# Expert rows gathered in quarters and transposed on VectorE: one change to a fused mixer and mixture-of-experts kernel

## The reference, cut to what matters

```python
probs = softmax(x @ w_router)                  # (2048, 16)
# top-1 of 4 expert groups, then top-2 experts within it
gate = take(probs, eidx); gate = gate / sum(gate)
# rows sorted by expert and padded to blocks of 128 rows
hid = silu(xb @ w1[e]) * (xb @ w3[e])          # (128, 512)
y   = hid @ w2[e]                              # (128, 1024)
ffn = sum over the two experts of y * gate
out = layer_norm(ALPHA * h + ffn)
```

## Time and profile before

| What | Value |
|---|---|
| median of 3 runs | 2238.5 us |
| the three runs | 1352.0, 2238.5, 5668.24 us |
| span of the profiled execution | 1348.3 us |
| its own time, span and what lies around it | taken as the lowest run, 1352.0 us (3.7 us more than the span) |
| TensorE busy in the span | 1311.4 us (97%) |
| VectorE, ScalarE, GpSimd busy | 958.4, 511.7, 525.1 us |
| granted clock of TensorE, mean | 0.994 |
| the loop over blocks | from about 650 to 1335 us |

### The profile page before, as it was taken

How to read it: one execution, slowest core, us unless ns; L and a number is a source line. 1 busy time by engine, 2 the same in 40 slices (tenths; PEclk the granted TensorE clock), 3 DMA queues, 4 the chain that set the end, 5 groups by cost and what they waited for, 6 DMA issues and landing times. The chain is left out here.

```text
span 1348.3 us, 20368 instructions
## 1 busy us (share of the span) xinstructions
PE 1311.4 (97%) x6382; PEld 1095.8 (81%) x6383; DVE 958.4 (71%) x1357; ACT 511.7 (38%) x568; POOL 525.1 (39%) x543
## 2 busy tenths in 40 slices
PE   5999999999999999998999999999999999999995
PEld 5888888888888888887888888888888888888884
DVE  7758577687759785698777886665675677776564
ACT  3423234322443234323444454343443454434241
POOL 2001010111101110022566665755665656666555
PEclk9999999999999999999999999999999999999998
DMA  9625434563455344544777774563554545666421
GB/s 266 181 89 162 149 111 163 170 192 109 156 186 158 110 141 159 208 181 169 287 263 256 271 270 147 193 234 132 181 202 181 191 164 214 236 231 238 142 69 64
DMA packets 156522, 243.58 MB, mean 181 GB/s; under 512 B 18944, under 2 KB 84992, under 8 KB 156480
## 3 DMA queue, kind: packets, MB, share of 16 engines
q1 hardware_dynamic: 118624, 154.15, 35.3%
q0 software_dynamic: 28928, 71.74, 15.0%
q10 hardware_dynamic: 8928, 17.13, 3.7%
HBM read 211.97 MB, written 64.62 MB: 205 GB/s over the span
## 5 line engine op out<-in xcount | busy, mean ns | idle before, releaser
L520 PE MATMUL acc<-ring_hi 128*128 128x512 f32 (+1 forms) x800 | 308.8, 386 | 2.1 <-DVE ring_lo L1239 1.9
L522 PE MATMUL acc<-ring_hi,ring_lo 128*128 128x512 f32 (+1 forms) x800 | 305.6, 382 | 0.0
L521 PE MATMUL acc<-ring_lo,ring_hi 128*128 128x512 f32 (+1 forms) x800 | 305.3, 382 | 0.0
L520 PE MATMUL acc<-ring_hi,xt_hi 128*128 128x512 f32 x648 | 256.7, 396 | 4.1 <-issue 2.8
L522 PE MATMUL acc<-ring_hi,xt_lo 128*128 128x512 f32 x648 | 252.8, 390 | 0.0
L521 PE MATMUL acc<-ring_lo,xt_hi 128*128 128x512 f32 x648 | 252.4, 390 | 0.0
L1802 POOL TENSOR_TENSOR small<-small 128x1 f32<-128x1 f32 x31 | 47.4, 1527 | 360.8 <-DVE small L1208 360.8
L520 PEld LDWEIGHTS acc<-ring_hi 128*128 128x128 f32 x800 | 151.3, 189 | 30.1 <-DVE ring_lo L1239 2.5
L522 PEld LDWEIGHTS acc<-ring_hi,ring_lo 128*128 128x128 f32 x800 | 151.2, 189 | 29.1
L521 PEld LDWEIGHTS acc<-ring_lo,ring_hi 128*128 128x128 f32 x800 | 151.3, 189 | 27.7
L921 ACT CAST ring_hi<-stage_x 128x2048 fp32r<-128x2048 f32 x64 | 119.4, 1915 | 76.3 <-PE acc L522 75.8
(11 more groups left out here) (276 smaller groups left out, 1884.0 us busy)
## 6 DMA issues: line engine op xcount, KB each, us to landing
stage_x<-in_exp_w SPq DMA_DIRECT2D x64, 1024.0 KB, 6.2
stage<-in_w_in SPq DMA_DIRECT2D x64, 512.0 KB, 5.4
stage<-in_exp_w SPq DMA_DIRECT2D x32, 1024.0 KB, 6.6
stage<-in_w_out SPq DMA_DIRECT2D x32, 512.0 KB, 5.3
h_scratch<-hres POOLq DMA_DIRECT2D x16, 512.0 KB, 3.0
sum_scratch<-hres ACTq DMA_DIRECT2D x16, 512.0 KB, 2.9
hrow<-in_x POOLq DMA_DIRECT2D x12, 512.0 KB, 4.8
h_scratch<-hrow POOLq DMA_DIRECT2D x12, 512.0 KB, 3.0
```

The lines of the kernel that those rows point to most:

```text
L520: nc.tensor.matmul(dst, w_hi, x_hi, start=start, stop=False)
L521: nc.tensor.matmul(dst, w_hi, x_lo, start=False, stop=False)
L522: return nc.tensor.matmul(dst, w_lo, x_hi, start=False, stop=stop)
```

## The change

`h1_dram` now holds rows of 1024 elements and is also read as 8192 rows of 256 (`h1_quarters`). The gates go to 16 extra columns of `sum_dram`. For the blocks from the third on, the gather of 128 rows becomes four gathers of 128 quarter rows. They are placed so that VectorE's transposes of 32x32 blocks (`x_turn`) put them in the order that the matmuls want, into a new SBUF buffer `xt`; the weights `w1` and `w3` are loaded in the matching order, `(p k)` for `(k p)`. `x_hi` and `x_lo` read `xt` and no longer PSUM. The indices of the quarters are made once (`spread_tokens` on TensorE, `quarter_indices` on VectorE). `hid` is no longer multiplied by the gate; `final_sums` multiplies the w2 product with the gate column that the gather of the sums brought along, and a copy carries the 16 gates over to `rrow`. `gate_col` and its semaphore are gone. `table` row 1 holds one word with expert, `ends` and `ended`.

```diff
-    w1_v = exp_w1[0].rearrange("(g i) (k p) f -> i g p k f", p=P, g=NEG)
+    w1_v = exp_w1[0].rearrange("(g i) (p k) f -> i g p k f", p=P, g=NEG)
...
@@ TensorE, loop
                 up(e_of, 1, s_w3)
-                x_tile(b + 1)
                 pe_of = pe.value_load(table[0:1, 0, bass.ds(b - 1, 1)], min_val=0, max_val=NE - 1)
@@ TensorE, once, ahead of the loop
+            def spread_tokens():
+                pe.wait_ge(s_tok, 1)
+                pe.wait_ge(s_selset, 1)
+                pe.wait_ge(s_xtlo, 6)
+                for m in range(Q4):
+                    dst = tp[m // 2][:].rearrange("p q t -> p (q t)")[:, m % 2 * COLS:(m % 2 + 1) * COLS]
+                    mm = nc.tensor.matmul(dst, sel[:, m, :], tok[:], start=True, stop=True)
+                mm.then_inc(s_spread, 1)
@@ ScalarE, turn
-                e_of = act.value_load(table[0:1, 0, bass.ds(b, 1)], min_val=0, max_val=NE - 1)
-                e_next = act.value_load(table[0:1, 0, bass.ds(b + 1, 1)], min_val=0, max_val=NE - 1)
-                ends = act.value_load(table[0:1, 1, bass.ds(b, 1)], min_val=0, max_val=1)
+                word = act.value_load(table[0:1, 1, bass.ds(b, 1)], min_val=0, max_val=4 * NE - 1)
+                e_of, ends, ended = (word >> 2).with_bounds(min_val=0, max_val=NE - 1), word & 2, word & 1
...
-                gate_col(b + 1, e_next)
                 act.wait_ge(s_w3, b + 1)
-                x_hi(b + 1)
+                x_hi(b, first)
@@ VectorE
+            def x_turn(b):
+                dve.wait_ge(s_gatq, b * 64 - 64)
+                by_k = xq.rearrange("p m (c k) -> p k m c", k=KT)
+                for h in range(2):
+                    V.transpose(xt[:, 4 * h:4 * h + 4, :].rearrange("p k (m c) -> p k m c", m=Q4),
+                                by_k[:, 4 * h:4 * h + 4]).then_inc(s_xq, 1)
+
+            def x_lo(b, early=False):
                 for h in range(2):
                     dve.wait_ge(s_xthi, b * 2 + h + 1)
-                    V.tensor_tensor(xt_lo[:, 4 * h:4 * h + 4, :], tp[h][:], xt_hi[:, 4 * h:4 * h + 4, :].bitcast(F32),
+                    src = tp[h][:] if early else xt[:, 4 * h:4 * h + 4, :]
+                    V.tensor_tensor(xt_lo[:, 4 * h:4 * h + 4, :], src, xt_hi[:, 4 * h:4 * h + 4, :].bitcast(F32),
                                     ALU.subtract).then_inc(s_xtlo, 1)
@@ hid_rows
-                V.scalar_tensor_tensor(out=hid[:], in0=act_a[:], scalar=col, in1=acc[1][:], op0=ALU.mult,
-                                       op1=ALU.mult).then_inc(s_hid, 1)
+                V.tensor_tensor(hid[:], act_a[:], acc[1][:], ALU.mult).then_inc(s_hid, 1)
@@ final_sums
-                    ins = V.tensor_tensor(rrow[:, cols], srow[:, cols], acc[2 + n][:], ALU.add)
-                ins.then_inc(s_y, 1)
+                    V.scalar_tensor_tensor(out=rrow[:, cols], in0=acc[2 + n][:], scalar=srow[:, bass.ds(col, 1)],
+                                           in1=srow[:, cols], op0=ALU.mult, op1=ALU.add)
+                V.tensor_copy(rrow[:, D:ROW], srow[:, D:ROW]).then_inc(s_y, 1)
@@ VectorE, turn
                 with dve.If(ends > 0):
                     units_lo(e_of + 1, 0, (0,) if first else (0, 1))
+                if not first:
+                    x_turn(b)
                 hid_rows(b)
...
+                    quarter_indices()
@@ GpSimd
+            def gather_quarters(b):
+                if isinstance(b, int):
+                    pool.wait_ge(s_xt, 6)
+                else:
+                    pool.wait_ge(s_xq, b * 2 + 4)
+                pool.wait_ge(s_gn, b + 4)
+                carry(pool, s_pool_past)
+                for m in range(Q4):
+                    G.indirect_dma_start(xq[:, m, :], None, h1_quarters,
+                                         bass.IndirectOffsetOnAxis(ap=gat_now[:, m:m + 1], axis=0),
+                                         bounds_check=Q4 * SEQ - 1, oob_is_err=False).then_inc(s_gatq, 16)
...
                 if rows:
-                    gather_rows(b + 3)
+                    gather_quarters(b)
```

More of the change, by code:

```diff
@@ L27 @@
 I32 = mybir.dt.int32
+I16 = mybir.dt.int16
 U32 = mybir.dt.uint32
@@ L64 @@
 ROW = D + NE
+Q4 = 4
+QW = D // Q4
 ALIGN = 128
@@ L414, in build @@
         s_xt = sem("x_transposed")
+        s_gatq = sem("quarters_gathered")
+        s_xq = sem("quarters_transposed")
+        s_tok = sem("token_columns")
+        s_spread = sem("tokens_spread")
+        s_selset = sem("select_set")
+        s_quart = sem("quarter_indices")
         s_xthi = sem("x_t_hi")
@@ L585, in pool_map, with x_transpose @@
                     .then_inc(s_pm, 1)
+            def x_transpose(rows, banks=tp):
+                by_k = rows.rearrange("p (c k) -> p k c", k=KT)
+                for b in range(2):
+                    for q in range(4):
+                        mm = nc.tensor.transpose(banks[b][:, q, :], by_k[:, 4 * b + q, :], ident[:])
+                    mm.then_inc(s_xt, 1)
             def h1_tile(c, t):
@@ L1090, in _, with x_hi @@
             act.wait_ge(s_xt, 2)
-            act.wait_ge(s_gcol, 1)
             split_hi_expert(0, EU - 1)
-            def x_hi(b):
+            def x_hi(b, early=False):
                 for h in range(2):
-                    act.wait_ge(s_xt, b * 2 + h + 1)
-                    nc.scalar.copy(xt_hi[:, 4 * h:4 * h + 4, :], tp[h][:]).then_inc(s_xthi, 1)
-            def gate_col(b, e_of):
-                act.wait_ge(s_gat, b * 16 + 16)
-                nc.scalar.copy(gate[:, bass.ds(b, 1)], xg[:, bass.ds(e_of + D, 1)]).then_inc(s_gcol, 1)
+                    if early:
+                        act.wait_ge(s_xt, b * 2 + h + 3)
+                        src = tp[h][:]
+                    else:
+                        act.wait_ge(s_xq, b * 2 + h + 1)
+                        src = xt[:, 4 * h:4 * h + 4, :]
+                    nc.scalar.copy(xt_hi[:, 4 * h:4 * h + 4, :], src).then_inc(s_xthi, 1)
             def hid_hi(b):
@@ L1162, in _ @@
             hid_hi(0)
-            gate_col(1, 0)
-            x_hi(1)
+            x_hi(0, True)
             silu(1)
@@ L1171, in _ @@
                 turn(b, False)
-            ended = act.value_load(table[0:1, 1, bass.ds(nb1 - 1, 1)], min_val=0, max_val=1)
+            ended = act.value_load(table[0:1, 1, bass.ds(nb1, 1)], min_val=0, max_val=4 * NE - 1) & 1
             hid_hi(nb1 - 1)
@@ L1650, in units_lo, with quarter_indices, final_sums @@
                                     ALU.subtract).then_inc(s_elo[w], 1)
-            def final_sums(b):
+            def quarter_indices():
+                dve.wait_ge(s_spread, 1)
+                for h in range(2):
+                    ins = V.tensor_scalar(quarter_of[:].rearrange("p c m -> p m c")[:, 2 * h:2 * h + 2, :],
+                                          tp[h][:].rearrange("p q t -> p (q t)").rearrange("p (m c) -> p m c", m=2),
+                                          float(Q4), quarter, ALU.mult, ALU.add)
+                ins.then_inc(s_quart, 1)
+            def final_sums(b, col):
                 at0 = isinstance(b, int) and b == 0
@@ L1714, in turn @@
             def turn(b, first, split=True):
-                e_of = dve.value_load(table[0:1, 0, bass.ds(b, 1)], min_val=0, max_val=NE - 1)
-                ends = dve.value_load(table[0:1, 1, bass.ds(b, 1)], min_val=0, max_val=1)
-                if not first:
-                    ended = dve.value_load(table[0:1, 1, bass.ds(b - 1, 1)], min_val=0, max_val=1)
-                    if split:
-                        hid_lo(b - 1)
+                word = dve.value_load(table[0:1, 1, bass.ds(b, 1)], min_val=0, max_val=4 * NE - 1)
+                e_of, ends, ended = (word >> 2).with_bounds(min_val=0, max_val=NE - 1), word & 2, word & 1
+                if not first and split:
+                    hid_lo(b - 1)
                 with dve.If(ends > 0):
                     units_lo(e_of + 1, 0, (0,) if first else (0, 1))
+                if not first:
+                    x_turn(b)
                 hid_rows(b)
-                x_lo(b + 1)
+                x_lo(b + 1, first)
                 with dve.If(ends > 0):
@@ L1731, in turn @@
                     hid_lo(b)
-                final_sums(b - 1)
+                    quarter_indices()
+                final_sums(b - 1, D if first else (e_of - ended + D).with_bounds(min_val=D, max_val=ROW - 1))
                 final_rows(b - 1)
@@ L1738, in turn_last @@
             def turn_last(b, prev):
-                ended = dve.value_load(table[0:1, 1, bass.ds(b - 1, 1)], min_val=0, max_val=1)
+                ended = dve.value_load(table[0:1, 1, bass.ds(b, 1)], min_val=0, max_val=4 * NE - 1) & 1
                 hid_lo(b - 1)
@@ L1744, in turn_last @@
                                 xt_hi[:, 0:FT, :].bitcast(F32), ALU.subtract).then_inc(s_htlo, 1)
-                final_sums(prev)
+                final_sums(prev, (ROW - 1 - ended).with_bounds(min_val=D, max_val=ROW - 1))
                 with dve.If(ended > 0):
```

103 lines of the change are left out of this document (58 added, 45 removed).

## The result

The changed kernel takes 1378.2 us (median of 4 runs, 1375.9 to 1381.7); the kernel before takes 1350.4 and 1352.0 us in its two runs that agree with its profile (its other two took 2238.5 and 5668.2 us and are left out). The ratio is 1.0206, with a 95% interval of 1.0192 to 1.0221: slower clear of noise, though not clearly by more than 2%. The forecast was 1346 us, so the change is 26 us slower where 6 us of gain were expected. The time lies near the upper end of the range (1384), between the rivals "GpSimd is held up by `xt_lo`" (1367 us) and "the gathers cost their upper bound" (1390 us).

A forecast was written before the change was run, and what follows sets the result against it. TensorE was taken to bound the loop: 34.4 us gained, 23.1 given back by GpSimd, 2 lost ahead of the loop, about 3 in VectorE's six turns, leaving 6 us: 1352.0 to 1346 us, 8-in-10 range 1320 to 1384.

The forecast's parts named there:

- GpSimd is held up by `xt_lo`: At GpSimd's index copies, half of `xt_lo`'s 1.29 us lost each turn: 1367 us, at the full 1.29 us 1390; chance 0.15.
- the gathers cost their upper bound: Four gathers ahead of the put, at 1.60 us each, slide onto the splits of `w2`: 1390 us; chance 0.15.
- The gain of TensorE: Eight transposes leave TensorE in each of the loop's 37 turns, 0.93 us a turn: 34.4 us.
- GpSimd's budget: GpSimd's free time in the loop, 107.9 us with 8.1 us of allowed lateness, against 131 us of gathers: 23 us given back.
- The price of a gather: Each of 111 added gathers on GpSimd takes 1.18 us, between 1.04 and 1.60, with next to no gap: 131 us.
- point of decision: The gather price, 1.53 us, from which the rival of gathers at their upper bound ends slower.
- the 2 us ahead of the loop: Four small matmuls and `quarter_indices` added ahead of the loop, with the first gathers waiting: 2 us, between nothing and 5.
- The cost of a transpose: Two VectorE transposes of 128x512 added to each turn at 0.680 us each, 1.275 us as upper bound.
- VectorE's six turns: Where two experts' splits adjoin, VectorE has no gap; turns get 1.64 us longer instead of 0.93 us shorter: 15.4 us.
- The 47.5 us ahead of the bias: GpSimd's wait for ScalarE ahead of adding the bias, counted wholly as free time.
- the 97.8 us: GpSimd's wait ahead of the put of the sums, 37 times, counted as free time except 11.1 us of gaps.

The follow-up runs named there:

- the fifteenth run: The thirteenth kernel with one gather of whole rows and the transposes on TensorE, as in the kernel before: 1354.4 us.
- run 16: The thirteenth kernel with VectorE's transposes reading 32 adjacent elements, which leaves the column order wrong: 1328.0 us.
- the thirteenth: Changed kernel with scale and bias in one VectorE operation, GpSimd's three index copies moved to where nothing waits for them, `hid` ahead of the transposes: 1338.0 us.
- run 2: Changed kernel with three of the four gathers in each turn, the fourth quarter of the rows left out: 1338.6 us.
- run 3: Changed kernel with a fifth indirect gather of 128 x 16 elements into unused columns behind the four: 1434.0 us.
- run 7: Changed kernel with VectorE's transposes reading 32 adjacent elements instead of every eighth, which leaves the column order wrong: 1371.7 us.
- run 1: Changed kernel with one of the four gathers in each turn, the other three quarters of the rows left out: 1353.8 us.
- run 6: Changed kernel with VectorE's transposes written to PSUM, so that `xt_lo` has one SBUF input instead of two: 1383.0 us.
- run 8: Changed kernel with scale and bias in one VectorE operation, rows scattered after the next block's gathers, `hid` ahead of the transposes, these writing PSUM: 1408.0 us.
- 11: Changed kernel with GpSimd's addition of the bias on 16 of 1024 columns in every block but the first: 1365.7 us.

## Why the prediction was wrong, step by step

**The gain of TensorE** (34.4 us) was real and a little too large: 29.6 us of busy time go (runs 15 and 16). Against the fifteenth run, the thirteenth shows 16 us of it in time and the sixteenth 26 us. In the changed kernel none of it arrives.

**GpSimd's budget** (107.9 us) fits the result, in part by luck. The change adds 114 gathers, not 111. With the price that the five gathers gave: 114 x 1.47 = 168 us of work, 60 given back, 34.4 - 60 - 2 = -27, and 1352 + 27 = 1379 us. Measured: 1378.2. But for three gathers the same working gives 76 x 1.47 = 112 us and 1323 us, where run 2 took 1338.6. The budget took GpSimd's other instructions as fixed, and they were not. From 660 to 1320 us, before and after, `frstd` took 55.3 and 31.7 us, the addition 104.1 and 89.2, the gather of the sums 62.2 and 48.2, and the copies `put_now` and `sum_now` 23.0 and 53.5 us (the changed kernel has one or two turns fewer in that stretch). With the 1.63 us of the rows and the other terms as they stood, the sum would be some 19 us too high.

**The price of a gather is the step that failed**: "I take 1.18 us each, ... with next to no gap, because no wait stands between the four". It is 1.33 + 0.30 = 1.63 us by the rows, and in time 1.47 us for a fifth gather (run 3) and 1.04 us for the fourth (run 2). The gap of 0.30 us was in the earlier trace rows and had been put down to the waits ahead of it; in the changed kernel it lies ahead of each further gather of a set. The mean of 1.301 us in the earlier trace rows was the one to take too, as the mean afterwards is 1.329. The bound above was at hand, and the middle of the bounds had no row behind it. The rival that used the bound had the mechanism and the place right: gathers slide onto VectorE's splits, as at 1051.52 and 1053.72 us, where they take 1.9 us. Its point of decision, 1.53 us, leaves out the 2 us ahead of the loop; with them it is 1.51 us.

**The cost of a transpose** was mis-sized too: 1.159 us for 0.680. An operation of the same size that reads with a stride was priced like one that reads densely. In the changed kernel this is worth 6.5 us (run 7), and once GpSimd is in time 10 us (run 16). The Trainium skill, "SBUF — State Buffer", section "Door 1: The DMA port swizzle", says that consecutive elements in one 16-byte line of SBUF come at full rate and that each new line costs extra, which puts the free reach for fp32 at four elements; the 0.687 us dense and 1.16 us at a stride of eight agree.

**VectorE's six turns**: 15.4 us forecast, 15.5 us of waits for `hid` measured once GpSimd was in time (run 1). That the two agree is luck: with the transposes at their 1.14 us the same working gives 6 x 3.50 = 21.0 us, against 15.5 + 3.9 = 19.4 us of waits for `hid` and `xt_lo`. The place was right. That these waits also cost clock was missing.

**The rival on `xt_lo`** had the contention right and the victim of this pair wrong. `xt_lo` and GpSimd's addition of the bias, in the changed kernel:

```profile
1042.18 2.40 POOL L1978 TENSOR_TENSOR orow<-arow,b 128x1024 f32<-128x1024 f32 x1
...
1043.39 2.35 DVE L1605 TENSOR_TENSOR xt_lo<-xt,xt_hi 128x512 fp32r<-128x512 f32 x2
```

The addition kept its 2.40 us, the pair of `xt_lo` took 2.35 us instead of 1.29. It was VectorE that was held up. The Trainium skill, "SBUF — State Buffer", section "Who interferes with whom", says that the port pair which VectorE and GpSimd share is an exclusive lock, and that the order of issue decides who blocks. These rows agree: the addition came first. GpSimd was held up as well, but elsewhere: its copies `put_now` and `sum_now` took 0.81 and 0.70 us instead of 0.44 and 0.18, and of the 47 us in such copies of over 0.5 us all but some 5 lay beside VectorE's splits of `w1` and `w3` and not beside `xt_lo`. No term of the prediction had that. Run 6 shows that taking the contention away brings no time while GpSimd is the limit.

**A wait is not only free time.** The 47.5 us ahead of the bias and part of the 97.8 us were counted as free. As a budget for more work this was right. The opposite reading, that work taken away is time gained, is not: below them lie the landings of the three indirect DMAs of a block, which runs 8 and 11 uncovered.

What stays open: the rest between 1328 us (run 16) and the 1317 us at which TensorE alone would end, and why a gather costs 1.04 us in time as the fourth and 1.47 us as the fifth, of which only a part is placed above.

## What to carry to other kernels

Price an instruction that is to be repeated back to back by its pitch, with the gap ahead of it, and by its mean among the work beside which it will run, not by its undisturbed duration; where only bounds are known, take the row of the same kind and not the middle. Before work is taken off an engine that issues DMAs, look for the index or buffer that is used again only when its last DMA has landed: that wait takes the place of the work unless the reuse is moved as well. Where TensorE sets the end and is made to wait, it may lose clock behind the wait, so the wait can cost more than its length.

## What the runs showed of the hardware

- Indirect DMAs issued back to back by GpSimd: 1.00 to 1.06 us each and 0.30 us between, about the same for 1024, 4096 and 16 bytes a row; beside VectorE's splits and `nrow` single gathers took longer, the longest 3.12 us (changed kernel).
- Their landing is late beside that: medians of 4.6 us from issue to landing for the gather of the sums and 3.3 us for the output rows (run 8):

```profile
srow<-sum_scratch,sum_now POOLq DMA_INDIRECT x35, 4.6
out<-arow,out_now POOLq DMA_INDIRECT x34, 3.3
```

- VectorE's transposes of 32x32 blocks, 128x512 in float32 from SBUF: 0.687 us with dense reads and 1.14 to 1.16 us with a stride of eight elements; into PSUM 1.152 us (run 6), no faster.
- TensorE fell to the 1.2 GHz level (128x512 matmuls every 0.42 instead of 0.23 us) behind each of the six waits of 2.5 to 2.7 us in run 1. In the changed kernel it did so behind one single wait of 1.49 us and behind five pairs of waits with the transposes of `hid` between them (one of 0.76 and 2.48 us, the others of 0.8 to 1.3 us each). Three other pairs and eight single waits of 1.6 to 1.9 us had no slow matmuls behind them. With single waits of up to 1.4 us in the loop (run 2) its granted clock stayed at 1.00.
